# Relative-position bias tables of a grid attention layer: 64 small DMA loads from HBM in place of 8 line loads and an expansion on GpSimd

## The reference

```python
GRID_W, NA_KH, NA_KW, C_HEADS, HEAD_DIM = 64, 8, 16, 16, 128
# rows = 256 / 64 = 4, so kh = min(8, 4) = 4 and every query row sees all 4 key rows
dc = clip(col[None, :] - col[:, None] + NA_KW - 1, 0, 2 * NA_KW - 2)
rpb_cols = rpb[:, :, dc]                       # rpb: (16 heads, 15, 31)
dr = r0 + arange(kh) - r + NA_KH - 1
bias = rpb_cols[:, dr]
sc = einsum('bqhd,bkwhd->bhqkw', q_r, k_r) * scale + bias
sc = where(col_mask, sc, -1e30)                # 16 key columns around each query column
p = softmax(sc)
y = einsum('bhqkw,bkwhd->bqhd', p, v_r) * silu(z)
x = x + y @ w_out
```

## Time and profile before

| | |
|---|---|
| median of 3 runs | 1900.34 us (1897.25 to 1901.09) |
| the profiled execution | 1901.09 us |
| its span | 1899.3 us |
| TensorE busy | 1863.8 us, 98% |
| VectorE busy | 1007.8 us, 53% |
| ScalarE busy | 865.3 us, 46% |
| GpSimd busy | 173.2 us, 9% |
| moved by DMA | 339.17 MB, mean 179 GB/s |

### The profile page before, as it was taken

One profiled execution on the slowest core, in us unless ns is written; L12 is line 12 of the kernel. 1 busy time (PEld: TensorE's weight loads), 2 busy tenths in 40 slices (PEclk: granted clock), 3 DMA queues, 4 the chain that ended last, 5 costly groups with the idle time before them and its releaser, 6 DMA issues.

```text
span 1899.3 us, 24183 instructions
## 1 busy us (share of the span) xinstructions
PE 1863.8 (98%) x9570; PEld 1591.3 (84%) x9570; DVE 1007.8 (53%) x991; ACT 865.3 (46%) x1075; POOL 173.2 (9%) x166
## 2 busy tenths in 40 slices
PE   6999999999899999999999999999999999999998
PEld 5889988798688998879887888888888888888886
DVE  4535554474654456446566555455455545545544
ACT  6334553464454445337454444354344434445443
POOL 1400011000331001100011000010000101100011
PEclk9999999999999999999999999999999999999999
DMA  8754555355556455445555554455555555456453
GB/s 294 216 179 150 170 181 174 122 182 198 178 187 209 150 172 186 145 157 173 178 177 200 195 203 163 163 177 174 188 189 185 181 167 183 153 177 199 165 190 111
DMA packets 186086, 339.17 MB, mean 179 GB/s; under 512 B 6512, under 2 KB 47856, under 8 KB 185072
## 3 DMA queue, kind: packets, MB, share of 16 engines
q1 hardware_dynamic: 179840, 313.81, 49.9%
q0 software_dynamic: 5264, 20.60, 3.8%
q10 hardware_dynamic: 864, 3.15, 0.4%
HBM read 335.43 MB, written 2.10 MB: 178 GB/s over the span
## 4 chain that ended last, share of the span: by engine, by line
PE 94%; DVE 2%; ACT 2%; DMA 1%; issue 1%; SPq 0%; ACTq 0%; DVEq 0%
PE acc L1433 27%; PE acc L1435 27%; PE acc L1434 27%; PE bank L1550 3%; PE bank L1490 1%; DMA raw<-in_w_in 1%; PE bank L1519 1%; PE bank L1539 1%; PE bank L1749 1%; PE bank L1477 1%; DVE w_lo L930 1%; ACT w_hi L616 1%; PE bank L1653 1%; PE bank L1521 0%; DVE xt_lo L975 0%
## 5 line engine op out<-in xcount | busy, mean ns | idle before, releaser
L930 DVE TENSOR_TENSOR w_lo<-raw,w_hi 128x2048 fp32r<-128x2048 f32 (+4 forms) x308 | 674.4, 2192 | 596.1 <-ACT w_hi L616 595.9
L1433 PE MATMUL acc<-w_hi,xt_hi 128*128 128x512 f32 (+4 forms) x2464 | 937.0, 380 | 19.2 <-DVE xt_lo L975 13.1
L1435 PE MATMUL acc<-w_hi,xt_lo 128*128 128x512 f32 (+4 forms) x2464 | 928.8, 377 | 0.0
L1434 PE MATMUL acc<-w_lo,xt_hi 128*128 128x512 f32 (+4 forms) x2464 | 928.1, 377 | 0.0
L616 ACT ACTIVATE w_hi<-raw 128x2048 fp32r<-128x2048 f32 (+4 forms) x308 | 557.3, 1812 | 629.7 <-PE acc L1435 601.3
L1433 PEld LDWEIGHTS acc<-w_hi,xt_hi 128*128 128x128 f32 x2464 | 463.8, 188 | 101.8 <-DVE xt_lo L975 15.0
L1435 PEld LDWEIGHTS acc<-w_hi,xt_lo 128*128 128x128 f32 x2464 | 463.5, 188 | 82.0
L1434 PEld LDWEIGHTS acc<-w_lo,xt_hi 128*128 128x128 f32 x2464 | 464.0, 188 | 79.8 <-issue 0.5
L683 ACT ACTIVATE S<-S,nmax 128x256 f32<-128x256 f32 (+1 forms) x128 | 59.9, 469 | 75.1 <-DVE nmax L1022 50.1
L492 POOL DMA_DIRECT2D bias<-in_b_in x32 | 17.8, 557 | 615.5 <-DVE M L1010 184.9
L670 ACT ACTIVATE PT<-bank 128x512 f32<-128x512 f32 (+4 forms) x78 | 36.8, 551 | 70.5 <-PE bank L1539 52.4
(11 more groups left out here) (266 smaller groups left out, 1130.4 us busy)
## 6 DMA issues: line engine op xcount, KB each, us to landing
raw<-in_w_in SPq DMA_DIRECT2D x80, 1024.0 KB, 4.9
raw<-in_w_in_c SPq DMA_DIRECT2D x64, 1024.0 KB, 5.3
raw<-in_w_in_ab SPq DMA_DIRECT2D x52, 1024.0 KB, 4.9
raw<-in_w_out SPq DMA_DIRECT2D x32, 1024.0 KB, 5.1
raw<-in_w_out_ab SPq DMA_DIRECT2D x16, 1024.0 KB, 5.1
raw<-in_w_out_c SPq DMA_DIRECT2D x16, 1024.0 KB, 5.1
raw<-in_w_in SPq DMA_DIRECT2D x16, 688.0 KB, 3.9
raw<-in_w_in SPq DMA_DIRECT2D x16, 576.0 KB, 3.6
```

The source lines that it names most:

```text
L930: nc.vector.tensor_tensor(w_lo[r][:, :, 0:n], raw[r][:, :, 0:n], w_hi[r][:, :, 0:n].bitcast(F32), ALU.subtract).then_inc(lo_done.s, 1)
L1433: nc.tensor.matmul(s, xt_hi[:, kt, rows], w_hi[r][:, k, 0:n], start=(q == 0 and k == 0), stop=False)
L1434: nc.tensor.matmul(s, xt_hi[:, kt, rows], w_lo[r][:, k, 0:n], start=False, stop=False)
L1435: ins = nc.tensor.matmul(s, xt_lo[:, kt, rows], w_hi[r][:, k, 0:n], start=False, stop=(q == NQ - 1 and k == KQ - 1))
```

## The change

The line, its loads and the four additions go. Instead, for each of 4 heads and each of 4 grid rows r a DMA reads from HBM, for 64 partitions, 4 pieces of 64 floats that lie 31 floats apart, and writes them straight into the table: 16 DMAs of 64 KB a batch, 64 in all, each with 64 x 4 = 256 source rows of 256 bytes. They are issued from GpSimd's queue when VectorE has read the last table. GpSimd waits for all 16, then adds the column mask in place with one instruction over 128 x 2048, and VectorE waits for that one. The loads of the line were issued one batch ahead; these are issued within the batch's own turn. The tiles TW and KR move from the space that later layers use again into space of their own.

```diff
--- before.py
+++ after.py
@@ -76,11 +76,6 @@
 CAUSAL_W = P + SEQ
 
 
-GRID_W, BACK_H, BACK_W = 64, 15, 31
-GRID_ROWS = SEQ // GRID_W
-LINE_W = BACK_W * (2 * (T - 1) + GRID_ROWS - 1) + GRID_W
-
-
 CONST = {}
 _at = 0
 for _name, _n in (("ident", P), ("causal", CAUSAL_W), ("tri_le", P), ("ones", P), ("tri_ge", P),
@@ -141,11 +136,13 @@
         w_hi = [sb(f"w_hi{r}", [P, KQ, CW], F32R) for r in range(RING)]
         w_lo = [sb(f"w_lo{r}", [P, KQ, CW], F32R) for r in range(RING)]
         TQ, TK, TV = sb("TQ", [P, T, GW]), sb("TK", [P, T, GW]), sb("TV", [P, T, GW])
+        TW = sb("TW", [P, T, 268])
         CT = sb("CT", [P, T, GW])
         S = sb("S", [P, HB, T, SEQ])
         PT = sb("PT", [P, HB, T, SEQ])
         gT = sb("gT", [P, KT_N])
         side = sb("side", [P, 3 * 768])
+        KR = sb("KR", [P, T, MLA_R])
         tmp = sb("tmp", [P, GW])
         bias = sb("bias", [P, CW])
         cst = sb("cst", [P, CONST_W])
@@ -182,12 +179,8 @@
             ukv = hybrid_sb("ukv", [P, HB * 2 * HD])
             QR = hybrid_sb("QR", [P, T, HB * MLA_R])
             mla_g = hybrid_sb("mla_g", [P, GW])
-            TW, KR = hybrid_sb("TW", [P, T, 268]), hybrid_sb("KR", [P, T, MLA_R])
 
         QT_hi, QT_lo, KT_hi, KT_lo = (sb(name, [P, HB, SEQ], F32R) for name in ("QT_hi", "QT_lo", "KT_hi", "KT_lo"))
-
-
-        line = sb("line", [P, HB, LINE_W])
 
         acc = [[ctx.enter_context(nc.psum_tensor(f"acc{i}{t}", [P, CW], F32)) for t in range(T)] for i in range(2)]
         bank = [ctx.enter_context(nc.psum_tensor(f"bank{i}", [P, 512], F32)) for i in range(4)]
@@ -274,8 +267,8 @@
         z_out, z_neg, z_soft, r_sub = chain("sb_step", HB, HB, HB, HB)
         z_exp, z_ln, r_exp = chain("sb_exp", HB, HB, HB)
         z_masked = signal("z_masked", 2)
-        table_in, table_masked = signal("table_in", 16), signal("table_masked", HB)
-        rpb_in = signal("rpb_in", 16 * 2)
+        table_in, table_masked = signal("table_in", 16), signal("table_masked", 1)
+        rpb_in = signal("rpb_in", 16 * 16)
         sink_max, sink_gap, sink_exp = signal("sink_max", 2), signal("sink_gap", 1), signal("sink_exp", 1)
         z_gate, xg_done, out_dve, out_act = signal("z_gate", T), signal("xg_done", 0), signal("out_dve", 0), signal("out_act", 0)
         stored = signal("stored", 0)
@@ -571,28 +564,20 @@
             for b in range(1, 4):
                 pool.wait_ge(*att.biased(b - 1, HB))
                 nc.gpsimd.dma_start(table, ab_table[b].rearrange("p (h t s) -> p h t s", h=HB, t=T)).then_inc(table_in.s, 16)
-            def load_line(b):
-                for half in range(2):
-                    rows = slice(GRID_W * half, GRID_W * half + GRID_W)
-                    src = bass.AP(rpb_back.tensor, rpb_back.offset + HB * b * BACK_H * BACK_W + (GRID_ROWS + half) * BACK_W - 48,
-                                  [[1, GRID_W], [BACK_H * BACK_W, HB], [1, LINE_W]])
-                    nc.gpsimd.dma_start(line[rows], src).then_inc(rpb_in.s, 16)
-
-            load_line(0)
+            GR = 64
             for b in range(4):
-                pool.wait_ge(*rpb_in(b, 16 * 2))
                 pool.wait_ge(*att.biased(HB + b - 1, HB))
                 for h in range(HB):
-
-
-                    at = line[:, h, :]
-                    shifted = bass.AP(at.tensor, at.offset, [list(at.ap[0]), [2 * BACK_W, T], [BACK_W, GRID_ROWS], [1, GRID_W]])
-                    nc.gpsimd.tensor_tensor(table[:, h].rearrange("p t (k n) -> p t k n", n=GRID_W), shifted,
-                                            c("na").unsqueeze(1).unsqueeze(1).broadcast_to([P, T, GRID_ROWS, GRID_W]),
-                                            ALU.add).then_inc(table_masked.s, 1)
-                if b < 3:
-                    pool.wait_ge(*table_masked(b, HB))
-                    load_line(b + 1)
+                    for r in range(SEQ // GR):
+
+
+                        src = bass.AP(rpb_back.tensor, rpb_back.offset + (HB * b + h) * 15 * 31 + (4 + r) * 31 - 48,
+                                      [[1, GR], [31, SEQ // GR], [1, GR]])
+                        dst = table[GR * (r % 2):GR * (r % 2 + 1), h, r // 2, :].rearrange("p (k n) -> p k n", n=GR)
+                        nc.gpsimd.dma_start(dst, src).then_inc(rpb_in.s, 16)
+                pool.wait_ge(*rpb_in(b, 16 * 16))
+                rows = table.rearrange("p h t s -> p (h t s)").rearrange("p (a n) -> p a n", n=GR)
+                nc.gpsimd.tensor_tensor(rows, rows, c("na").unsqueeze(1).broadcast_to([P, HB * T * SEQ // GR, GR]), ALU.add).then_inc(table_masked.s, 1)
             pool.wait_ge(*att.biased(7, HB))
             nc.gpsimd.dma_start(gain, all_rows(ln_f)).then_inc(g_in.s, 16)
             pool.wait_ge(*g_in(DEPTH, 16))
@@ -1316,7 +1301,7 @@
                     for stage, b in stages.get(k, []):
                         g = batch0(turn) + b
                         if stage == "S":
-                            dve.wait_ge(*(table_in(b, 16) if turn == DEPTH else table_masked(b, HB)))
+                            dve.wait_ge(*(table_in(b, 16) if turn == DEPTH else table_masked(b, 1)))
                             scores_in(att, g, (2, 3, 0, 1), lambda h: table[:, h] if turn == DEPTH else table_back(h))
                             if turn == DEPTH and b < 2:
                                 dve.wait_ge(*att.biased(g, HB))
```

## The result

| | before | after |
|---|---|---|
| median | 1900.71 us (1897.25 to 1901.69, 4 runs) | 1919.34 us (1916.3 to 1926.46, 4 runs) |
| ratio | | 1.010, 95% interval 1.0082 to 1.0119 |
| span of the profiled execution | 1899.3 us | 1918.2 us |

The change costs 18.6 us, 1.0%. I had forecast 1900.5 us and no change, in a range up to 1905.5.

A forecast was written before the change was run, and what follows sets the result against it. TensorE, busy 98% of the span, was taken to bound the kernel. Removed work gained 0 and added work cost 0, so 1901.09 + 0 = 1901, forecast as 1900.5 us, no change, range 1896.5 to 1905.5.

The forecast's parts named there:

- What bounds the kernel: TensorE, busy in 98% of the span; the edit matters only if it makes TensorE wait.
- deadline: In the grid layer, 72.5 us from VectorE's last read of the old table to its read of the new.
- issues: On GpSimd's queue, 16 loads a batch at 0.62 us each, 10 us together.
- table: Table ready at about 1531 to 1537, at worst 1544, against 1577.4; at least 33 us left, cost 0.
- rival A: GpSimd's loads go one at a time, the table comes after 98 us and VectorE waits; 1965 us, chance 0.03.
- The sum of the transfers: A batch's table loads on 16 DMA engines: 5 us by bytes, 17 us by packets; 12 us taken.
- What the loads disturb: Weight loads behind the score stage may land late, but TensorE doesn't wait; cost 0 to 1 us.
- The add: One GpSimd add, taken as 5.5 us, can hold up one w_lo within 8.1 us of cover; cost 0.
- The clock: TensorE at full granted clock in all 40 slices; the sum has no term for a lower clock.
- Rival B: Table packets dearer than the line's starve the weights, TensorE loses 12 us four times; 1948 us, chance 0.09.
- Rival C: Adds leave the crowded stretch behind the score stage, four batches give back 4 us; 1896.5 us, chance 0.03.

The follow-up runs named there:

- e11: Changed kernel reading other values: true 256-byte rows, a partition's pieces 4 KB apart, partitions 256 bytes apart; 1901.32 us.
- e2: Changed kernel with all 64 loads but without the mask addition, a one-column write in its place; 1910.20 us.
- e3: Changed kernel with at most two of the 16 loads in flight, same loads and same single add; 1900.71 us.
- e4: Changed kernel reading other values: each partition's kilobyte is one contiguous 1 KB row, partitions 4 bytes apart; 1900.14 us.
- e1: Changed kernel with the mask added by four instructions of 128x512, one a head, instead of one of 128x2048; 1908.74 us.
- e12: Changed kernel reading other values: true 256-byte rows, a partition's pieces 4 KB apart, partitions 4 bytes apart; 1901.20 us.
- e13: Changed kernel reading other values: true 256-byte rows, pieces 4 KB apart, all 64 partitions reading the same four rows; 1899.75 us.
- e5: Changed kernel reading other values: rows at multiples of 256 bytes, partitions 256 bytes apart, in effect rows of 1 KB; 1900.38 us.
- e10: Changed kernel reading other values: aligned rows, in effect of 1 KB, all 64 partitions of a load reading the same place; 1900.59 us.
- e6: Changed kernel with at most four of the 16 loads in flight; 1900.96 us.

## Why the prediction was wrong

**What bounds the kernel, deadline, issues, table:** right. Issue was 9.8 us for 10, the add 4.6 us for 5.5, the table stood ready at least 35 us ahead of its read, and rival A didn't come.

**The sum of the transfers:** near the dear end. That end was 270 engine-us and the value taken 12 x 16 = 192; measured are 224 to 316. That the dear end came close was luck, for its two factors were both wrong: 1280 packets of 0.21 us were forecast, and it was 512 (6672 on GpSimd's queue in all, not 9744) of 245 / 512 = 0.48 us. The line loads, too, read small rows from one place, and e11 shows that 4096 rows alone would have cost 66.

**What the loads disturb: this step failed.** I let the first weight load pass 32 table packets of 0.21 us, 6.7 us, to land in 12 us, and put the cost at 0 to 1 us. The mechanism was right, the price of a packet was not: 5.2 + 32 x 0.48 = 20.6 us is what the same formula gives with the measured price, and 20.6 us is what the load took in the batch of 1588. (The 32 are all the table packets that an engine has, not part of 80; half of them are of 4 KB and dear, 245 engine-us over 16 engines and 16 packets, up to 1.0 us each.) So the first weight load landed only at the end of the burst. That the formula hits the number is in part luck, for it takes all 16 engines as alike. The DMA view of 1594 to 1614.6 us, in which this load was under way, speaks against that:

```profile
q0 software_dynamic: 440, 0.87, 49.6%
q1 hardware_dynamic: 1313, 2.62, 37.1%
```

The weights' queue moved 2.62 MB, two and a half loads, before the first load of 1 MB was complete. So it seems that some engines had long gone on to the next loads while others still held the first one up; no view shows the engines one by one. Instead of 0 to 1 us the late weights alone cost about 10 us (e2), and with the add and the clock behind them 18.6. The limit that I had worked out for it, 18 us from its issue, was right: in e2, with no add beside it, a load that took 21.5 us stopped TensorE for 3.39, which puts the limit at 18.1. That bytes are gathered into large packets could have been read from the kernel before. Its DMA view of 1115 to 1125 us has the table load of the banded layer, 1 MB, in 144 packets:

```profile
q0 software_dynamic: 144, 1.05, 30.8%
```

**The add:** "Cost 0" was worked out with 8 us of cover, and that cover was the weights' too. It was right where the weights were on time (e3, e4). Behind late weights one add of 4.6 us cost 9 us in the medians (1919.3 against e2's 1910.2), and four short ones, of 1.3 us each at the median, nothing (e1, 1908.7). I priced two disturbances of one cover each by itself. What the Trainium skill says of the shared port ("SBUF — State Buffer", Who interferes with whom) is borne out, with 4.55 and up to 6.73 us for a w_lo beside the add, which takes 2.29 by itself.

**The clock:** left out of the sum, about 5 of the 20.9 us. The page of before has TensorE's granted clock in its highest tenth in every slice, and I took a stop to cost its own length. After the stop of 4.68 us it was granted 0.51 for 5 us.

**Rival B** was what came: weights late at a place where VectorE is served late too. I gave it 0.09 and 1948 us. Its margin, "0.21 against 0.25", was called thin in the text and should have carried more than that; where it decides by a fifth of an unknown, even odds would have been honest. **Rival C** had nothing in it: the stretched w_lo of before cost nothing.

**What stays open:** why rows from one place are dear. Rows of 256 bytes cost twice as much from one place (e12, e13 against e11), rows of 1 KB that begin 4 bytes apart about 1.7 times (e4 against e5), rows of 1 KB all the same hardly more (e10). The runs give these conditions, not the mechanism. Also open is what makes GpSimd pause after 12 or 14 loads in two of four batches, and why eight in flight cost twice what sixteen do. No version was faster than the kernel before; pacing the loads (e3, e6) or lines of 876 bytes loaded a batch ahead and expanded by GpSimd are equal in time.

## What to carry to other kernels

Ask of a transfer that is hidden by its own deadline what shares the DMA engines with it: a burst that is not late itself can still make the stream late on which TensorE lives, and its damage is the length of the backlog. Keep few loads in flight when the deadline is far; two or four at a time cost nothing here, sixteen at once 1%, and eight, whose bursts were longer but unbroken, 2%. And count a stretch of cover once: two disturbances that are each hidden may not be hidden together. A stop of TensorE can cost more than its length: behind some stops here the granted clock was lower for a while (0.51 and 0.81 behind the one of 4.68 us), behind others it stayed at 1.00 (those of 2.44 and 2.78 us).

## What the hardware showed that I had not expected

- Reading 64 KB out of one place of 880 bytes in rows of 256 bytes took the DMA engines about four times as long (224 to 316 engine-us a batch) as reading the same number of rows of the same size from places apart (59 to 69). Rows of 1 KB all from the same place didn't (60 to 69), and rows of 1 KB that begin 4 bytes apart lay between (88 to 109).
- Source pieces that lie end to end were issued like one row: the shortest issue of 4 x 64 floats that lie 64 apart took 0.53 us, and of those 31 or 1024 apart 0.62 us. Rows of every size came in 512 packets a batch, 256 of them of 4 KB.
- Eight loads in flight were worse than sixteen issued at once (1940 against 1919 us), and four in flight cost nothing (1901).
